# Order of the first loads in a hybrid decoder step: the first cache gather ahead of the compression weights and the input tiles

## What is computed

```python
def compress(rows, pe, w1, w2):
    ...
    proj = jnp.einsum('bnkf,rfh->rbnkh', chunks, w1.reshape(r_n, CMP_STRIDE * HEAD_DIM, CMP_HIDDEN))
    pre = sum(proj[r][:, r:r + nc] for r in range(r_n)) + pe.reshape(-1) @ w1
    out = jax.nn.silu(pre) @ w2
...
def adaln(c, w_ada, b_ada):
    mod = jax.nn.silu(c) @ w_ada + b_ada
...
def gather_past(pool, page_table, new_rows):
    old = pool[page_table].reshape(b, -1, N_KV_HEADS, HEAD_DIM)
```

## Time and profile before

| | kernel before |
|---|---|
| median of three runs | 1075.23 us (1066.83 to 1075.36) |
| profiled execution, its own time | 1075.33 us |
| its span | 1073.5 us |
| mean granted clock of TensorE | 0.965 of full |
| TensorE busy | 998.8 us (93% of the span) |
| VectorE, ScalarE, GpSimd busy | 479.1, 348.6, 105.7 us |
| DMA | 134.09 MB, mean 125 GB/s |

### The profile page before, as it was taken

How to read it: one execution, slowest core, us unless ns; L and a number is a source line. 1 busy time by engine, 2 the same in 40 slices (tenths; PEclk the granted TensorE clock), 3 DMA queues, 4 the chain that set the end, 5 groups by cost and what they waited for, 6 DMA issues and landing times.

```text
span 1073.5 us, 16168 instructions
## 1 busy us (share of the span) xinstructions
PE 998.8 (93%) x6572; PEld 815.1 (76%) x6572; DVE 479.1 (45%) x992; ACT 348.6 (32%) x662; POOL 105.7 (10%) x146
## 2 busy tenths in 40 slices
PE   2999999999988887788979999999999998999998
PEld 2877877999856555356643489999999998776776
DVE  1456772689357774554432462222222223333533
ACT  2464552221333334355720342222222223223120
POOL 3112000000022211233500130000000000000000
PEclk9899999999898998688989999999999999999999
DMA  7987422162555774650100162222222223112301
GB/s 250 368 305 233 143 76 86 40 252 68 177 202 187 291 308 169 239 148 1 32 1 17 62 186 80 79 79 79 79 79 79 79 79 118 39 63 76 104 0 45
DMA packets 59062, 134.09 MB, mean 125 GB/s; under 512 B 4979, under 2 KB 33219, under 8 KB 52590
## 3 DMA queue, kind: packets, MB, share of 16 engines
q1 hardware_dynamic: 51298, 90.76, 25.3%
q0 software_dynamic: 7264, 42.18, 11.0%
q10 hardware_dynamic: 428, 0.13, 0.1%
HBM read 128.23 MB, written 8.95 MB: 128 GB/s over the span
## 4 chain that ended last, share of the span: by engine, by line
PE 82%; DVE 7%; DMA 4%; ACT 3%; issue 3%; POOL 0%; SPq 0%; ACTq 0%; DVEq 0%
PE bank L1811 18%; PE bank L1812 18%; PE bank L1813 18%; PE bank L1805 8%; PE bank L2299 7%; PE bank L1878 5%; DMA arena<-in_cache_k_slc,idx 2%; PE bank L2150 2%; PE bank L1837 2%; PE bank L2269 1%; DMA rowb<-in_pe_cmp 1%; DVE uvT L1608 1%; PE bank L1887 1%; PE bank L2074 1%; ACT hbuf L1056 1%
## 5 line engine op out<-in xcount | busy, mean ns | idle before, releaser
L1811 PE MATMUL bank<-hlo,ws 128*128 128x288 f32 x704 | 208.2, 296 | 0.0
L1813 PE MATMUL bank<-hhi,ws 128*128 128x288 f32 x704 | 208.1, 296 | 0.0
L1812 PE MATMUL bank<-hhi,ws 128*128 128x288 f32 x704 | 207.7, 295 | 0.0
L458 DVE TENSOR_TENSOR ws<-wring,ws 128x1024 fp32r<-128x1024 f32 (+2 forms) x72 | 100.7, 1430 | 115.7 <-ACT hhi L455 50.7
L455 ACT CAST ws<-wring 128x1024 fp32r<-128x1024 f32 (+2 forms) x74 | 86.8, 1210 | 155.9 <-PE bank L1813 155.9
L1812 PEld LDWEIGHTS bank<-hhi,ws 128*128 128x128 f32 x704 | 132.7, 188 | 0.0
L1811 PEld LDWEIGHTS bank<-hlo,ws 128*128 128x128 f32 x704 | 132.2, 188 | 0.1
L1813 PEld LDWEIGHTS bank<-hhi,ws 128*128 128x128 f32 x704 | 132.2, 188 | 0.0
L1779 DVE TENSOR_TENSOR arena<-bank,uvT 128x288 f32<-128x288 f32 x44 | 20.1, 458 | 198.5 <-PE bank L1813 198.5
L1805 PE MATMUL bank<-cst,arena 128*128 128x128 f32 (+1 forms) x556 | 77.0, 293 | 15.6 <-DVE small L1500 4.7
L1812 PE MATMUL bank<-ws,hhi 128*128 128x512 f32 (+3 forms) x240 | 91.4, 381 | 0.0
(11 more groups left out here) (305 smaller groups left out, 1660.5 us busy)
## 6 DMA issues: line engine op xcount, KB each, us to landing
wring<-in_w_gu SPq DMA_DIRECT2D x44, 512.0 KB, 6.0
wring<-in_w_ada SPq DMA_DIRECT2D x16, 1024.0 KB, 10.4
wring<-in_w_in SPq DMA_DIRECT2D x10, 1024.0 KB, 5.0
wring<-in_w_down SPq DMA_DIRECT2D x10, 1024.0 KB, 5.1
wring<-in_w_ada SPq DMA_DIRECT2D x16, 512.0 KB, 9.5
proj<-in_x_prompt SPq DMA_DIRECT2D x4, 512.0 KB, 9.4
mem<-in_state_k_win POOLq DMA_DIRECT2D x8, 256.0 KB, 9.6
mem<-in_state_v_win POOLq DMA_DIRECT2D x8, 256.0 KB, 7.8
```

Of the source, the lines that this page charges most:

```text
L458: return eng.tensor_tensor(dst, src, hi.bitcast(F32), ALU.subtract)
L1811: pe.matmul(dst, sh, ml, start=first and k == 0, stop=False)
L1812: pe.matmul(dst, sl, mh, start=False, stop=False)
L1813: ins = pe.matmul(dst, sh, mh, start=False, stop=last and k == len(pairs) - 1)
```

## The change

It touches only the first stage. SyncE loads the page-table column of sequence 0 first, then the condition vectors, then the other seven columns; ScalarE's queue begins with the load of `cst`. `idx` is made for sequence 0 alone (which serves gathers 0 and 1), and for the others after VectorE's copies of chunk 0. GpSimd issues gather 0 ahead of `w_ck1`, and `w_cv1` and `w2` behind gather 2. Input tiles 0, 1 and 2 each wait for gathers 0, 1 and 2 to land. TensorE starts with chunk 0; the condition vectors and the small rows are turned behind chunk 1. The position rows of keys and values alternate, those of values in the upper 64 columns of the array and partitions of the bank. The condition vectors lie in `hbuf`, so that they don't share room with the first chunk's copies, and their silu stands behind the loads of `rowb`.

```diff
@@ plan_banks
-    start += [("cT",), ("rows",)]
     start += [("xt", 0, i) for i in range(4)]
     for u in range(16):
         if u < 15:
             start += [("xt", u + 1, i) for i in range(4)]
+        if u == 0:
+            start += [("cT",), ("rows",)]
@@ SyncE
-            pages_load(sp, (1,))
+            pages_load(sp, (0,))
             sp.dma_start(crow[0:1, :], a["c_prompt"]).then_inc(c_loaded, 16)
             sp.dma_start(crow[1:9, :], a["c_sample"]).then_inc(c_loaded, 16)
+            pages_load(sp, range(1, 8))
...
             for t in range(5):
-                if t == 2:
-                    pages_load(sp, range(2, 8))
-                if t == 3:
-
-                    cache(sp, 0)
+                if t < 3:
+
+                    cache(sp, t)
@@ GpSimd
-            hidden_load(0)
             pool.wait_ge(idx_ready, 1)
...
+                if i == 1:
+                    hidden_load(0)
                 if i == 2:
+                    pool.wait_ge(idx_ready, 2)
+                if i == 3:
                     hidden_load(1)
...
-                if i == 4:
-                    pool.wait_ge(idx_ready, 2)
@@ ScalarE
-            pages_load(act, (0,))
             act.dma_start(cst[:, 0:C_ROPE], a["consts"][:, 0:C_ROPE]).then_inc(ident_loaded, 16)
-            act.wait_ge(c_loaded, 32)
-            act.activation(scrow, crow, ACT.Silu).then_inc(scrow_ready, 1)
...
+            act.wait_ge(c_loaded, 32)
+            act.activation(scrow, crow, ACT.Silu).then_inc(scrow_ready, 1)
@@ VectorE
-            dve.wait_ge(first_pages_loaded, 32)
-            indices(0, 2)
+            dve.wait_ge(first_pages_loaded, 16)
+            indices(0, 1)
...
             spread(0)
+            dve.wait_ge(pages_loaded, 112)
+            indices(1, 8)
@@ TensorE
+            def turn_rows():
+                pe.wait_ge(scrow_ready, 1)
...
             def position_rows():
 
                 pe.wait_ge(comp_w_loaded, 64)
+                want_emptied(pe, ("cT",))
                 want_emptied(pe, ("rows",))
...
+                for i in range(16):
+                    for x in range(2):
+                        ins[x] = pe.matmul(ps(("peb", x))[64 * x:64 * x + 64, 0:1], w1v[:, x, i % 8, i // 8, :], colT[:, 36 + i:37 + i],
+                                           start=i == 0, stop=i == 15)
...
                 if u < 15:
                     turn_chunks(u + 1)
                 if u == 0:
+                    turn_rows()
                     pe.wait_ge(comp_k_loaded, 32)
```

More of the change, by code:

```diff
@@ L289, in decoder_kernel @@
         cpg = uvT[0:NC, 2056:2088].rearrange("p (a q) -> p a q", a=4)
-        crow, scrow = uvT[0:9, 0:D], uvT[0:9, D:2 * D]
+        crow, scrow = hbuf[0:9, 2 * D:3 * D], hbuf[0:9, D:2 * D]
         sgb = uvT[:, 0:2 * TOK].rearrange("p (s n) -> p s n", s=2)
@@ L528, in pages_load @@
                 eng.dma_start(pti[:, b:b + 1], bass.AP(a["page_table"].tensor, 16 * b, [[1, 16], [0, 8], [1, 1]])
-                              ).then_inc(first_pages_loaded if b < 2 else pages_loaded, 16)
+                              ).then_inc(pages_loaded if b else first_pages_loaded, 16)
         block = ctx.enter_context(nc.Block())
@@ L1169, in indices @@
                                          ALU.mult, ALU.add).then_inc(idx_ready, 1)
-            dve.wait_ge(first_pages_loaded, 32)
-            indices(0, 2)
-            evac(("cT",), cT[:, :].rearrange("p (k r) -> p k r", r=32)[:, :, 0:9],
-                 ps(("cT",))[:, 0:72].rearrange("p (k r) -> p k r", r=9))
+            dve.wait_ge(first_pages_loaded, 16)
+            indices(0, 1)
             def x_normed(t):
@@ L1203, in low_job1 @@
                 ins.then_inc(lo1_ready, 1)
-            evac(("rows",), colT[:, :], ps(("rows",))[:, 0:52])
             def first_modulated():
@@ L1251, in _ @@
                 if u == 0:
-                    dve.wait_ge(pages_loaded, 96)
-                    indices(2, 8)
+                    evac(("cT",), cT[:, :].rearrange("p (k r) -> p k r", r=32)[:, :, 0:9],
+                         ps(("cT",))[:, 0:72].rearrange("p (k r) -> p k r", r=9))
+                    evac(("rows",), colT[:, :], ps(("rows",))[:, 0:52])
                     for x in range(2):
-                        evac(("peb", x), pebt[:, x:x + 1], ps(("peb", x))[0:64, 0:1])
+                        evac(("peb", x), pebt[:, x:x + 1], ps(("peb", x))[64 * x:64 * x + 64, 0:1])
                 if u == 7:
@@ L1816, in _ @@
             pe.wait_ge(ident_loaded, 16)
[L1817 to L1820, removed]
             def mod_turn(l):
@@ L1842, in ada_step @@
                     ins.then_inc(ada_read, 1)
-            pe.wait_ge(gains_loaded, 96)
-            fills(turn(ps(("rows",))[:, 0:52], rowb[:, :]), ("rows",))
+            def turn_rows():
+                pe.wait_ge(scrow_ready, 1)
+                want_free(pe, ("cT",))
+                for k in range(8):
+                    ins = turn(ps(("cT",))[:, 9 * k:9 * k + 9], scrow[:, 128 * k:128 * k + 128])
+                fills(ins, ("cT",))
+                pe.wait_ge(gains_loaded, 96)
+                want_free(pe, ("rows",))
+                fills(turn(ps(("rows",))[:, 0:52], rowb[:, :]), ("rows",))
             def position_rows():
                 pe.wait_ge(comp_w_loaded, 64)
+                want_emptied(pe, ("cT",))
                 want_emptied(pe, ("rows",))
                 for x in range(2):
[L1852 to L1857, removed]
+                    want_free(pe, ("peb", x))
+                ins = [None, None]
+                for i in range(16):
+                    for x in range(2):
+                        ins[x] = pe.matmul(ps(("peb", x))[64 * x:64 * x + 64, 0:1], w1v[:, x, i % 8, i // 8, :], colT[:, 36 + i:37 + i],
+                                           start=i == 0, stop=i == 15)
+                for x in range(2):
+                    fills(ins[x], ("peb", x))
             def turn_chunks(u):
@@ L1907, in turn_tokens @@
                     fills(ins, key)
-            want_emptied(pe, ("cT",))
             turn_chunks(0)
```

## The result

The changed kernel takes 1078.59 us (median of 20 runs, 1072.26 to 1086.81), against 1069.41 us for the kernel before in 20 runs (1061.32 to 1080.26). The ratio is 1.0092, 95% interval 1.0069 to 1.0116: slower by 9 us, clear of the scatter. Each ratio in this document leaves out the runs of a kernel that lie over 1.5% above its fastest, so it needn't be the quotient of the medians beside it, and the kernel before was run again beside each variant, with medians from 1068.28 to 1069.41 us. The forecast was a gain of 1.5 us, with 1078.5 us as the upper end. The measured median lies only 0.1 us beyond that end, but the median of before over 20 runs is 5.8 us lower than that of the three runs known at the time: what was to be a gain of 1.5 us is a loss of 9.2.

The account below looks back on a forecast made before the run. TensorE, busy 93% of the span, was taken as the bound. Position rows ending 1.5 us earlier cut the span from 1073.5 to 1072.0 us, with 1.8 outside it 1073.8, stated as 1073.7; range 1066 to 1078.5.

Parts of the forecast that it names:

- Gather 0 lands at 14.2: First gather on GpSimd's queue: issued at 6.3 us, landing at about 14.2 (12.2 to 19), where before it landed at 20.1.
- The term of the way (7.9): Gather 0 from issue to landing: 4.7 us start cost plus 3.2 us for 1 MB at 324 GB/s.
- Gather 1 at 17.8, turn 1 without a wait: Gather 1, issued at 9.9 us, lands at about 17.8, in time for TensorE's turn 1, which ends at 20.9.
- The wait for the weights of the position rows, 4.9 us: TensorE, ready at 25.8 us, waits 4.9 us for `w_cv1` and `w2`, issued at 23.7 and landing at 30.7.
- the forecast (a): The main case: TensorE's wait moves to the weights of the position rows and most idle time stays; 42%.
- Position rows 3.3 us: Alternating position rows on TensorE take 3.3 us instead of 5.08, mostly at low clock with some overlap; bounds 1.8 and 6.4.
- P1: The end of the position rows on TensorE: forecast at 34.0 us instead of 35.45, 1.5 us gained.
- The `w_ada` tile, landing at 40, "just in time": Weight tile for the first `ada_step`: issued at about 26.5 us, 13.5 us under way, needed at 41.3.
- Rival (c): Slower: the `w_ada` tile binds, landing at 45.0 us ahead of the first `ada_step`; 2.3 us lost, 1077.6 us; 20%.
- (d): Rival: TensorE isn't throttled after the position rows, turn 2 costs 1.90 us instead of 3.60; 1071.8 us; 10%.
- What P2 gains the whole kernel gains: P2 is the start of the first `ada_step`, forecast 41.3 us instead of 42.73; its gain carries to the end.
- the hidden things: Index columns, silu, bank order and room for condition vectors: end before 20 us, used by TensorE at 20.9 or later.

Follow-up runs that it names:

- the experiment with two columns: Changed kernel with the page columns of sequences 0 and 1 loaded first and made into `idx` together: 1079.13 us, ratio 1.0101 to the kernel before.
- the old pacing: Changed kernel with SyncE's input tiles 0 to 2 without a wait and one wait for gather 0 ahead of tile 3: 1080.15 us, ratio 1.0100.
- cut kernels: Kernels ended where the projection would begin, so only the first stage runs and no output is written: kernel before 146.73 us, changed kernel 155.05 us.
- the kernel before with the new pacing: Kernel before with page columns in one piece ahead of the input tiles, and input tiles 0 to 2 behind gathers 0 to 2: 1071.93 us, ratio 1.0024.

## Why the prediction was wrong, point by point

- **Gather 0 lands at 14.2**: it was issued at 4.30 (I took 6.3, with 4.2 as the lower bound) and landed 7.4 us later, at 11.7. `cst` came in 1.9 us instead of 5.3, and the index waited for the page column of 3.0 us, not for `cst`. That the loads beside it had made the 5.3 is likely, but not shown by itself, since `cst` now also stands first in its queue. The term of the way (7.9) was right within 0.5 us. 2.5 us better than forecast, just outside my range on the early side.
- **Gather 1 at 17.8, turn 1 without a wait**: wrong. It took 12.2 us from 7.66, and TensorE waited 4.5 us, until 19.9. I gave it the price of gather 0, though it has `w_ck1` ahead and the page columns beside it. The two errors cancelled only in part: product 0 was to start at 22.3 and started at 24.73, then at low clock.
- **The wait for the weights of the position rows, 4.9 us**: it didn't occur. They were issued at 22.7 (23.7 expected), and the 16 KB landed 6.3 us later, at 29.0 (30.7). TensorE reached them only at 30.44, since product 0 took 5.78 us at low clock. So the start of the position rows was right (30.44, where 30.7 was forecast) by luck: another path set it, and the wait on which the forecast (a) rests wasn't there.
- **Position rows 3.3 us**: 2.03, near the lower bound, at full clock. The Trainium skill (TensorEngine Tiling (Array Packing), Theoretical Speedup) with its up to 2x is borne out at 1.75x: the records cost 32 ns, the ones of before 56 at full clock. P1 = 32.4, predicted 34.0, before 35.45.
- **The `w_ada` tile, landing at 40, "just in time"**: this is the step that failed. The tile landed at 47.7. Issue at 26.5, measured 27.74: from the issue of gather 2 to that of the tile I left 6.5 us, and it was 8.4 (6.90 for the gather, 1.48 for the issues of three input tiles, where I counted two). For the way I took 13.5 us, less than the 16.1 of before, and argued that less stood beside it. It was 19.9. Two things follow from the new order that I passed over: the tile has 1.25 MB of its own queue right in front (before it was 0.75 MB and the rest of a tile that landed at 23.3), and three more gathers of 1 MB, at 23.61, 24.93 and 26.20, are issued within the 4 us ahead of it. The windows of the two queues from 26.3 to 47.7 us have 4.42 MB of the gathers' queue and 3.45 MB of SyncE's:

```profile
q0 software_dynamic: 706, 4.42, 57.0%
q1 hardware_dynamic: 655, 3.45, 44.6%
```

  With 16.1 us kept, the tile would have come at 42.6 by my own time of issue, which leaves 0.1 us of the gain, and at 43.8 by the measured one, which is a loss of 1.1. Rival (c) named this mechanism, at 45.0 and 2.3 us lost, with 20%. Its place was right; its way was 3.8 us too short and its issue 1.2 us too late, so that the landing lacked 2.7 us, and it lacked the clock.
- **The clock behind a stall** was missing from every rival. The 5.0 us of delay became 9.1, since TensorE ran the next 8.5 us at half its clock. I had this only as a gain in (d), which did come true: turn 2 took 1.97.
- **What P2 gains the whole kernel gains**: P2 lost 5.0 us and the whole kernel 9.1, so it failed over the slow stretch. From turn 4 on it holds: 9.1 us at turn 4, 9.1 at the projection, 9.2 in the medians.
- **Gather 2** waited for the page columns until 18.92, 2.0 us beyond VectorE's copies. I had counted these columns among the hidden things. Its issue at 19.36 was near the forecast 20.0 by luck, since gather 0 was 2.5 us early and the columns 2.0 us late. It is a link of the chain that made the tile late, but the experiment with two columns shows that it wasn't worth anything alone.

A single trace of a whole kernel can be off by some 2 us at turn 4, which is enough to explain why the old pacing and the two page columns looked better there than in the medians. Turn 4 stands at 59.35, 55.15 and 55.74 us in the whole traces of the changed kernel, the two columns and the old pacing, and at 57.09, 56.66 and 54.93 in those of their cut kernels: the 4.2 us of the two columns shrink to 0.4, the 3.6 of the old pacing to 2.2. The intervals of the whole times agree with the medians of the cut kernels (+6.8 and +7.9 us).

What stays open is how the input tiles ahead and the gathers beside act together on the tile. Taking away the first brings its way from 20.5 to 11.1 us in the cut kernels, and the kernel before with the new pacing has it at 12.6 with the first kept, since its gathers are issued at other times; so the excess can't be divided between the two. No run changes the gathers alone in the changed kernel.

## What to carry to other kernels

When a load is moved or a wait put into a queue, follow the whole queue behind it down to the first load whose consumer has little slack, and price its way not lower than the trace has it, with the bytes that now stand ahead of it in the same queue and the transfers of other queues issued shortly before it; here the tile was in time with either alone (11.1 and 12.6 us), and both together made 19.9. A small slack of a late load (5.6 us here) is the first thing to look up, ahead of the gain at the start. And a stall of TensorE can cost more than its length: here the slow stretch behind it added 4.1 us to the 5.0 of the delay.

## What the runs showed of the hardware

- A load of 68 KB took 5.3 us with two input tiles and a weight load beside it and 1.9 us without, and 9.7 us in the cut kernel before with the same loads beside it as in the 5.3. A page column of 512 bytes took 3.0 us as the first load and 12.7 us when it was issued between two gathers.
- A 1 MB tile on SyncE's queue took 19.9 us with 1.25 MB ahead of it and three gathers issued in the 4 us before it, 11.1 us with the same gathers and without the 1.25 MB, and 12.6 us with the 1.25 MB ahead and the gathers issued 15 us before it or behind it.
- 64 records of 128x64 stationary tiles with one moving column cost 80 ns each in one column half (56 at full clock) and 32 ns each at full clock when they alternate between the halves.
- The mean granted clock goes with the whole time from run to run: in the 20 runs of the changed kernel from 0.959 at 1086.8 us to 0.975 at 1073.0 us, about 8 us for each hundredth.
